# Last embedding phase in two column halves, and weight slabs laid out by the host

## The chip, the cores and the metric

The kernel runs on the 8 cores of one Trainium2 chip. Every core runs the same program on its own tokens, with the same weights read from the chip's memory. The metric is the device time of one execution in microseconds (us), which is that of the slowest core. Lower is better.

## The reference, cut to what matters

Each core holds 1044 token columns (1024 prompt tokens, 2 tokens of context, 16 sample tokens, 2 of padding). The two layers of the trunk are rows of these steps, D = 2048 wide:

```
h = h + 0.5 * swiglu(rmsnorm(h), ffn1)      # hidden width 5632
h = h + mixer(rmsnorm(h))                   # layer 0: chunked gMLP, layer 1: short convolution
h = h + 0.5 * swiglu(rmsnorm(h), ffn2)
gate = sigmoid(rmsnorm(h) @ ple_w_gate[i])  # 2048 x 2048
h = h + gate * (p[i] @ ple_w_proj[i])       # 256 x 2048
...
y = rmsnorm(h, final_norm)                  # after layer 1 alone
```

The last two statements of layer 1 and the final norm are what the change is about. A norm needs the sum of squares over all 2048 channels of a token, but no other token.

## The kernel before, in words

The state h lies on the chip, channels on partitions, as 16 channel blocks of 128 x 1044 float32. All projections are matmuls with a 128x128 block of weights as the stationary operand and token columns as the moving one. Every instruction is issued in the order of the program on its engine, and semaphore waits come from a record of the memory that each instruction reads and writes (class `Sync`).

**Feed-forward phases** (`ffn`) use a seven-product scheme on 2x2 blocks, with 261 columns per matmul; their weights are already laid out by the host so that each partition's part of a load is contiguous.

**All other projections** ("std" entries of `plan`) read a slab per output block: 2048 x 128 weights of one output block (or 256 x 128 for `ple_w_proj`), float32 in memory, converted to bf16 by the load. The source of one slab is a strided cut of a row-major matrix, so the longest contiguous piece is 128 floats, 512 bytes. Three slots hold slabs. `wget` (L385) for entry i first issues the loads up to entry i + 2 (`wpump`), and all these loads are issued from the POOL queue (L371). The slot of entry i + 2 is that of entry i - 1, so that load waits on the queue for the matmuls of entry i - 1. Whatever else POOL has to do stands in the same queue.

**The embedding phase** (`ple`, L797) runs over 16 output blocks d. In each: the gate group of 16 x 3 matmuls of 348 columns into banks 0 to 2; three products on DVE with the norm's scale into `sig`; a sigmoid on ACT; the projection group of 2 x 3 matmuls into banks 3 to 5; three products on DVE into `pletmp`; one addition on DVE into h; a square on ACT (L454); one addition on DVE into `acc` (L455). In block 0 the norm of the phase (`norm_all`) is placed between matmuls 12 and 13 of the gate's 16 k-steps, over all 1044 columns.

**The end** (L1128 to L1139): after block 15 the final norm over 1044 columns (`norm_all`), then per channel block one 1044-wide product with gain and scale, 11 of them on DVE and 5 on POOL after a scaling on ACT, and a store of 128 x 1044 float32 for each from the SP queue.

Of the kernel before, what the change touches and what calls it, by code (L numbers as in the profile page):

```python
# [6 lines left out]
F32 = mybir.dt.float32  # L7
BF16 = mybir.dt.bfloat16
F16 = mybir.dt.float16
AF = mybir.ActivationFunctionType  # L10
ALU = mybir.AluOpType

D = 2048
DFF = 5632
NCH = 16
NF = 44
DPLE = 256
# [6 lines left out]
TH = 1044  # L24
NH = TH // 2
NS = NH // 2
# [6 lines left out]
EPS = 1e-6  # L33
# [7 lines left out]
G_FIN = 13  # L41
# [115 lines left out]
def build_program():  # L157
    nc = bass.Bass("TRN2", target_bir_lowering=False, dynamic_dma_scratch_size=SCRATCH)

    def din(name, shape):  # L160
        return nc.dram_tensor(name, list(shape), F32, kind="ExternalInput").ap()
# [12 lines left out]
    for nm in ("ffn1", "ffn2"):  # L174
        for l in range(2):
            wd[nm, "g", l] = din("%s_g%d" % (nm, l), (NF // 2, 128, 4096))
            wd[nm, "u", l] = din("%s_u%d" % (nm, l), (NF // 2, 128, 4096))
            wd[nm, "d", l] = din("%s_d%d" % (nm, l), (DFF * D,))
    wd["a_in"] = din("a_w_in", (1, D, 2 * D))
    wd["a_out"] = din("a_w_out", (1, D, D))  # L180
    wd["c_in"] = din("c_w_in", (1, D, 3 * D))
    wd["c_out"] = din("c_w_out", (1, D, D))
    wd["ple_g"] = din("ple_w_gate", (2, D, D))
    wd["ple_p"] = din("ple_w_proj", (2, DPLE, D))
    wst_in = din("wst_in", (128, 8 * 128))
    a_b_s = din("a_b_s", (1, 8, 128))

# [15 lines left out]
    def view(name, shape, dt, off):  # L203
        names[name] = names.get(name, 0) + 1
        return nc.alloc_sbuf_tensor_at("%s_v%d" % (name, names[name]), [128] + list(shape), dt, offset=off)
# [65 lines left out]
    def plan_ple(l):  # L271
        for d in range(NCH):
            plan_std("ple_g", l, 0, 16, d * 128)
            plan_std("ple_p", l, 0, 2, d * 128)
# [16 lines left out]
        plan_std("c_out", 0, 0, 16, d * 128)  # L291
    plan_ffn("ffn2", 1)
    plan_ple(1)

    with contextlib.ExitStack() as es:
        S = Sync(nc, es)
# [25 lines left out]
        def act(out, a, func, more=(), **kw):  # L322
            S.op("act", [a, *more], [out], lambda: nc.scalar.activation(out=out, in_=a, func=func, **kw))  # L323
# [4 lines left out]
        def store(key, dst, a):  # L328
            S.dma("sp", [a], [], key, lambda: nc.sync.dma_start(out=dst, in_=a))
# [12 lines left out]
        def wissue(early=None):  # L342
            i = wst["issued"] if early is None else early
            ent = plan[i]
            if i in place_of:
                wst["issued"] += 1
                return
            if ent[0] == "std":
                _, name, l, k0, nk, c0 = ent
                if plan[i - 1][0] == "ffn":  # L350
                    wst["nstd"] = 0
                s = wst["nstd"] % 3
                wst["nstd"] += 1
                t = view("wsl", [16, 128], BF16, SLOT[s])
                src = wd[name][l].rearrange("(k p) c -> p k c", p=128)[:, k0:k0 + nk, c0:c0 + 128]
                dst, key = t[:, 0:nk, :], ("wl", s)
            else:
                _, nm, kind, l, nk, j = ent
                if i == 0 or plan[i - 1][0] == "std":
                    wst["nffn"] = 0  # L360
                n = wst["nffn"]
                wst["nffn"] += 1
                s = (2, 0, 1)[n % 3]
                t = view("raw", [4, nk, 128], F16, RAW[s])
                if kind == "d":
                    f0, d = j
                    src = bass.AP(wd[nm, "d", l].tensor, f0 * 128 * D + d * nk * 512 * 128, [[nk * 512, 128], [1, nk * 512]])
                else:
                    src = wd[nm, kind, l][j]
                dst, key = t[:].rearrange("p a k c -> p (a k c)"), ("wr", s)  # L370
            S.dma("pool", [], [dst], key, lambda: nc.gpsimd.dma_start(out=dst, in_=src))  # L371
            for a, b in span_of(dst):
                owner[a:b] = i
            place_of[i] = t
            if early is None:
                wst["issued"] += 1
# [420 lines left out]
        def ple(l, xn, pT, mode):  # L797
            sig = [view("sig", [TH], F32, NEW[0] + i * VB) for i in range(2)]
            tmp = view("pletmp", [TH], F32, NEW[0] + 2 * VB)
            for d in range(NCH):  # L800
                ws = wget("std", "ple_g", l, 0, 16, d * 128)
                mm_group(ws, 16, xn, PA, tile_major=d > 0, mid=norm_all if d == 0 else None)
                if d > 0 and mode == "pe":
                    norm_mm(d - 1)
                sb = sig[d % 2]
                evac3(lambda ti, t0, tn: tt("dve", sb[:, t0:t0 + tn], bank(PA[ti], tn), rstdF[:, t0:t0 + tn], ALU.mult))
                act(sb[:], sb[:], AF.Sigmoid)
                ws = wget("std", "ple_p", l, 0, 2, d * 128)
                mm_group(ws, 2, pT, PB)
                nst["acc"] = acc_ple  # L810
                evac3(lambda ti, t0, tn: tt("dve", tmp[:, t0:t0 + tn], bank(PB[ti], tn), sb[:, t0:t0 + tn], ALU.mult))
                tt("dve", h[:, d, :], tmp[:], h[:, d, :], ALU.add)
                if d == NCH - 1 and l == 0:
                    ffn_begin()
                h_next(d)
                if mode == "pe":
                    norm_sq(d)
                else:
                    acc_sq(d)
            nst["pend"] = ("ffn", mode)  # L820

        def gmlp_setup(step, wmT, bias2, wsn, bsb, ident_f, tri_f):
            if step == 0:
                load(("g", 0), wsn[:].rearrange("p h t -> p (h t)"), wst_in)
                load(("g", 1), bsb[:].rearrange("p h t -> p (h t)"), bass.AP(a_b_s.tensor, 0, [[0, 128], [1, 8 * 128]]))
                load(("cst", 1), ident_f[:], identd)
                load(("cst", 2), tri_f[:], trid)
            elif step == 2:
                S.op("dve", [ident_f[:]], [ident_b[:]], lambda: nc.vector.tensor_copy(out=ident_b[:], in_=ident_f[:]))
                for hh in range(8):  # L830
                    tt("dve", wmT[:, hh, :], wsn[:, hh, :], tri_f[:], ALU.mult)
            elif step == 3:
                def emit():
                    last = None
                    for hh in range(8):
                        last = nc.tensor.matmul(ps[:, (S0, S1)[hh // 4], (hh % 4) * 128:(hh % 4 + 1) * 128], lhsT=ones_b[:],
                                                rhs=wmT[:, hh, :], start=True, stop=True)
                    return last
                S.op("pe", [wmT[:], ones_b[:]], [bank(S0), bank(S1)], emit)
                for c in range(NCH):  # L840
                    hh = c // 2
                    stt("dve", bias2[:, c, :], ps[:, (S0, S1)[hh // 4], (hh % 4) * 128:(hh % 4 + 1) * 128], gcol(G_LNB, c),
                        bsb[:, hh, :], ALU.mult, ALU.add, more=[gcol(G_LNB, c)])
# [279 lines left out]
        ffn("ffn2", 1, XA, HA)  # L1123
        pT = load_p(1, off + XNB)
        nst["spec"] = ("fin", G_FIN, None)
        ple(1, xn, pT, "acc")
        assert wst["used"] == len(plan)
        nst["pend"] = ("fin", "acc")  # L1128
        norm_all()

        yo = [view("yo", [TH], F32, AR + i * VB) for i in range(16)]
        for c in range(2, NCH, 3):
            act(yo[c][:], h[:, c, :], AF.Copy, more=[gcol(G_FIN, c)], scale=gcol(G_FIN, c))
        for c in range(NCH):
            if c % 3 == 2:
                tt("pool", yo[c][:], yo[c][:], rstdF[:], ALU.mult)
            else:
                stt("dve", yo[c][:], h[:, c, :], gcol(G_FIN, c), rstdF[:], ALU.mult, ALU.mult, more=[gcol(G_FIN, c)])
            store(("o", "y", c), y_out[c], yo[c][:])  # L1139
        S.finish()  # L1140
    return nc

# [10 lines left out]
def pair_blocks(w):  # L1153

    k, m = w.shape
    a = w.reshape(k // 256, 2, 128, m // 256, 2, 128)
    return np.ascontiguousarray(a.transpose(3, 2, 4, 1, 0, 5)).reshape(m // 256, 128, -1)


def down_blocks(w):  # L1160
# [86 lines left out]
```

How the kernel before makes its waits and increments, by code:

```python
    def _wait_all(self, eng, deps):  # L109
        kn = self.known[eng]
        for k, v in deps.items():
            if k == "pe" and eng == "pe":
                continue
            if kn.get(k, 0) >= v:
                continue
            self.engs[eng].wait_ge(self.sems[k], v)
            self._learn(eng, k, v)
# [15 lines left out]
    def op(self, eng, reads, writes, emit):  # L133
        rs, ws = self._spans(reads), self._spans(writes)
        self._waits(eng, rs, ws)
        inst = emit()
        self.cnt[eng] += 1
        inst.then_inc(self.sems[eng], 1)
        self._record(eng, self.cnt[eng], eng, rs, ws)
# [1 line left out]
    def dma(self, queue, reads, writes, semkey, emit):  # L141
        rs, ws = self._spans(reads), self._spans(writes)
        self._sem(semkey, "s_" + "_".join(str(k) for k in semkey))
        self._waits(queue, rs, ws)
        inst = emit()
        self.cnt[semkey] += 16
        inst.then_inc(self.sems[semkey], 16)
        self._record(semkey, self.cnt[semkey], queue, rs, ws)
        self.dma_events[semkey] = self.cnt[semkey]
```

## Time and profile before

| what | value |
|---|---|
| median of 3 runs | 4791.91 us (4788.62 to 5107.49) |
| profiled execution | 4784.54 us, span 4783.5 us on its slowest core |
| spans of the 8 cores | 4773.8 to 4783.5 us |
| mean granted TensorE clock | 0.98 of full |
| PE busy | 4552.1 us, 95% of the span |
| DVE, ACT, POOL busy | 64%, 26%, 12% |
| chain that ended last | PE 88%, DVE 5%, DMA 2%, ACT 2% |
| last embedding phase | 4585.2 to 4726.9 us (first gate matmul to the end of the last gate group) |
| the end after it | 4726.9 to 4783.5 us |

The busy shares say that TensorE (PE) is at work nearly all the time; DVE has slack on average, which says nothing of a single phase. The table's last two rows are places in the timeline of the slowest core; the rows further down show them.

### The profile page before, as it was taken

To read this page: it belongs to the slowest core of one execution; us is meant where nothing else is said; L and a number is where in the kernel's file an instruction comes from. 1 tells how busy PE (TensorE), PEld (TensorE's weight loads), DVE (VectorE), ACT (ScalarE), POOL (GpSimd) and SP (SyncE) were. 2 spreads that over 40 slices of the span, in tenths; PEclk is the share of its full clock that TensorE was granted. 3 is DMA by queue.
4 is the path that set the end of the run, shared out by engine and by line. 5 is a ranking of instruction groups with operands and counts; after the bars stand their busy time and mean duration, and the time that the engine had idled before them with its cause. 6 is when DMAs were issued, how large, how long until landed. Compare 5 with 4: busy or idle time off the path is not lost.

```text
span 4783.5 us, 93347 instructions; the slowest of 8 cores (4773.8 to 4783.5 us)
## 1 busy us (share of the span) xinstructions
PE 4552.1 (95%) x37150; PEld 3623.5 (76%) x37150; DVE 3063.8 (64%) x5317; ACT 1234.1 (26%) x1857; POOL 571.5 (12%) x707
## 2 busy tenths in 40 slices
PE   6999999997999999999999999999999999999985
PEld 4888888764668888886588888886666788888863
DVE  6666666635566666666766666665445666666666
ACT  3222222525122222225222222232001222222342
POOL 0100110110101101101101110111111011101022
PEclk8999999998999999999999999999999999999997
DMA  5444545573754445444735444446778454454356
GB/s 126 80 73 87 89 73 93 71 71 33 67 76 85 72 84 89 81 88 61 77 70 96 77 82 80 87 78 68 75 71 83 74 89 80 73 93 84 73 66 107
DMA packets 360810, 380.57 MB, mean 80 GB/s; under 512 B 311984, under 2 KB 312624, under 8 KB 337840
## 3 DMA queue, kind: packets, MB, share of 16 engines
q0 software_dynamic: 355744, 359.80, 50.4%
q1 hardware_dynamic: 4640, 14.81, 1.1%
q8 instruction: 303, 4.96, 0.4%
q14 instruction: 123, 1.01, 0.1%
HBM read 721.22 MB, written 8.96 MB: 153 GB/s over the span
## 4 chain that ended last, share of the span: by engine, by line
PE 88%; DVE 5%; DMA 2%; ACT 2%; issue 2%; DVEq 0%; POOL 0%; ACTq 0%; SPq 0%; POOLq 0%
PE ps L567 67%; PE ps L403 19%; DMA wsl_v<-ple_w_gate 1%; DVE buf_v L315 1%; DVE st_v L910 1%; DVE yo_v L315 1%; ACT vhb_v L919 0%; ACT tb_v L323 0%; DVE tb_v L311 0%; DMA raw_v<-ffn_g 0%; ACT L323 0%; DVE hop_v L311 0%; DVE nw_v L311 0%; DVE h_v L311 0%; DMA h_v<-xin 0%
## 5 line engine op out<-in xcount | busy, mean ns | idle before, releaser
L567 PE MATMUL ps<-xop_v,raw_v 128*128 128x261 f16 x11264 | 1382.1, 276 | 16.3 <-DVE xop_v L315 7.5
L567 PEld LDWEIGHTS ps<-xop_v,raw_v 128*128 128x128 f16 x11264 | 1102.9, 98 | 207.1 <-issue 25.6
L567 PE MATMUL ps<-xop_v,nw_v 128*128 128x261 f16 x8448 | 1059.6, 277 | 20.9 <-ACT ps L323 14.5
L567 PEld LDWEIGHTS ps<-xop_v,nw_v 128*128 128x128 f16 x8448 | 828.1, 98 | 163.9 <-issue 25.4
L403 PE MATMUL ps<-xn_v,wsl_v 128*128 128x348 bf16 x5376 | 825.0, 315 | 35.7 <-DVE sig_v L311 15.5
L403 PEld LDWEIGHTS ps<-xn_v,wsl_v 128*128 128x128 bf16 x5376 | 526.1, 98 | 328.0 <-issue 43.4
L567 PE MATMUL ps<-hop_v,raw_v 128*128 128x261 f16 x5632 | 725.0, 276 | 18.5 <-DVE h_v L311 9.9
L323 ACT ACTIVATE tb_v<-ps 128x522 f32<-128x522 f32 x696 | 417.8, 604 | 873.1 <-PE ps L567 872.5
L311 DVE TENSOR_TENSOR h_v<-ps,h_v 128x522 f32<-128x522 f32 (+1 forms) x736 | 494.4, 675 | 229.0 <-PE ps L567 136.4
L567 PEld LDWEIGHTS ps<-hop_v,raw_v 128*128 128x128 f16 x5632 | 545.5, 98 | 120.9 <-issue 30.0
L567 PE MATMUL ps<-hop_v,nw_v 128*128 128x261 f16 x4224 | 558.4, 276 | 10.0 <-ACT tb_v L323 7.8
L567 PEld LDWEIGHTS ps<-hop_v,nw_v 128*128 128x128 f16 x4224 | 409.9, 98 | 86.9 <-issue 19.6
L323 ACT ACTIVATE ps<-ps 128x522 f32<-128x522 f32 x312 | 183.8, 589 | 889.8 <-PE ps L567 825.4
L323 ACT ACTIVATE tb_v<-tb_v 128x522 f32<-128x522 f32 x352 | 224.2, 639 | 689.0 <-DVE tb_v L311 689.0
L311 DVE TENSOR_TENSOR tb_v<-ps,rstdF_v 128x522 f32<-128x522 f32 x172 | 120.7, 702 | 349.2 <-PE ps L567 349.2
L311 DVE TENSOR_TENSOR tb_v<-ps,tb_v 128x522 f32<-128x522 f32 x356 | 248.8, 699 | 113.8 <-PE ps L567 111.8
L311 POOL TENSOR_TENSOR h_v<-tb_v,h_v 128x522 f32<-128x522 f32 x160 | 181.6, 1135 | 1139.2 <-ACT tb_v L323 1134.1
L315 DVE SCALAR_TENSOR_TENSOR sgr_v<-tb_v,rstdF_v 128x522 f16<-128x522 f32 x352 | 244.7, 696 | 29.1 <-ACT tb_v L323 28.7
L311 DVE TENSOR_TENSOR hop_v<-ps,sgr_v 128x522 f16<-128x522 f32 x176 | 123.4, 701 | 197.7 <-PE ps L567 197.7
L311 DVE TENSOR_TENSOR h_v<-tb_v,h_v 128x522 f32<-128x522 f32 x180 | 126.6, 703 | 185.5 <-ACT tb_v L323 185.5
L403 PE MATMUL ps<-buf_v,wsl_v 128*128 128x348 bf16 x1536 | 232.1, 313 | 10.6 <-DVE buf_v L311 6.2
L323 ACT ACTIVATE sqt_v<-h_v 128x1044 bf16<-128x1044 f32 (+1 forms) x141 | 150.5, 1067 | 321.9 <-DVE h_v L311 321.6
(126 smaller groups left out, 2946.8 us busy)
## 6 DMA issues: line engine op xcount, KB each, us to landing
raw_v<-ffn_g POOLq DMA_DIRECT2D x88, 1024.0 KB, 8.9
raw_v<-ffn_u POOLq DMA_DIRECT2D x88, 1024.0 KB, 8.8
raw_v<-ffn_d POOLq DMA_DIRECT2D x96, 512.0 KB, 5.6
raw_v<-ffn_d POOLq DMA_DIRECT2D x64, 640.0 KB, 6.4
wsl_v<-c_w_in POOLq DMA_DIRECT2D x48, 512.0 KB, 7.0
wsl_v<-a_w_in POOLq DMA_DIRECT2D x32, 512.0 KB, 6.9
wsl_v<-ple_w_gate POOLq DMA_DIRECT2D x32, 512.0 KB, 6.9
y<-yo_v SPq DMA_DIRECT2D x16, 522.0 KB, 7.1
```

What stands on the lines that cost most here:

```text
L311: S.op(eng, [a, b], [out], lambda: e.tensor_tensor(out=out, in0=a, in1=b, op=op))
L315: S.op(eng, [a, b, *more], [out], lambda: e.scalar_tensor_tensor(out=out, in0=a, scalar=scalar, in1=b, op0=op0, op1=op1))
L323: S.op("act", [a, *more], [out], lambda: nc.scalar.activation(out=out, in_=a, func=func, **kw))
L403: last = nc.tensor.matmul(ps[:, pset[ti], 0:tn], lhsT=ws[:, k, :], rhs=rhs[:, k, t0:t0 + tn], start=(k == 0), stop=(k == nk - 1))
L567: last = nc.tensor.matmul(ps[:, 2 * s + a, 0:NS], lhsT=lhs[:, k, :], rhs=rhs[:, k, a * NS:(a + 1) * NS], start=(start and k == 0), stop=(k ...
L910: S.op("dve", [bank((S0, S1)[q // 2])], [st6[jj][:, q, :]], lambda q=q: nc.vector.bn_stats(out=st6[jj][0:n, q, :], in_=pv[q // 2][0:n, (q ...
```

## The change

The last embedding phase is replaced by `ple_last`. It walks over the 16 blocks twice, each time for one half of the token columns (522 of 1044). Each half-step has a gate group of 16 x 2 matmuls of 261 columns, alternating between banks 0, 1 and banks 2, 3, and a projection group of 2 x 2 matmuls in banks 4 and 5; the DVE and ACT work is of half width. Each slab is loaded twice, once in each pass (`plan_ple(1)` stands twice in the plan).

The final norm of the first half is placed inside the first gate group of the second pass. The outputs of the first half are made in half-steps 2 to 15 of the second pass: even channel blocks on DVE, odd ones with a scaling on ACT and a product on POOL, each followed by its store. For four blocks of the second half the scaling on ACT is made early. After the second pass only the second half's norm, 16 half-width products (12 on DVE, 4 on POOL) and 16 half-width stores are left.

For `a_w_in`, `a_w_out`, `c_w_in`, `c_w_out`, `ple_w_gate` and `ple_w_proj` the host now writes each slab as 128 contiguous rows, so that a partition's part is one piece of 8192 bytes (1024 bytes for `ple_w_proj`).

```diff
-    wd["a_in"] = din("a_w_in", (1, D, 2 * D))
+    wd["a_in"] = din("a_w_in", (1, 2 * NCH, 128, D))
...
     plan_ple(1)
+    plan_ple(1)
...
-                src = wd[name][l].rearrange("(k p) c -> p k c", p=128)[:, k0:k0 + nk, c0:c0 + 128]
-                dst, key = t[:, 0:nk, :], ("wl", s)
+                src = wd[name][l][c0 // 128]
+                dst, key = t[:, 0:nk, :].rearrange("p k c -> p (k c)"), ("wl", s)
...
+        def ple_last(xn, pT):
...
+            def last_norm(p):
...
+                for b, c0 in ((S0, a), (S1, a + NS)):
+                    S.op("pe", [acc_ple[:, c0:c0 + NS], mean_f[:]], [bank(b, NS)], lambda b=b, c0=c0: nc.tensor.matmul(
+                        bank(b, NS), lhsT=mean_f[:], rhs=acc_ple[:, c0:c0 + NS], start=True, stop=True))
+                for b, c0 in ((S0, a), (S1, a + NS)):
+                    tsc("dve", sF[:, c0:c0 + NS], bank(b, NS), EPS, ALU.add)
+                act(rstdF[:, sl], sF[:, sl], AF.Ln)
+                act(rstdF[:, sl], rstdF[:, sl], AF.Exp, scale=-0.5)
+                act(t[:, sl], rstdF[:, sl], AF.Square, scale=0.5 ** 0.5)
+                act(rstdF[:, sl], rstdF[:, sl], AF.Copy, scale=-1.0)
+                tt("dve", sF[:, sl], sF[:, sl], t[:, sl], ALU.mult)
+                stt("dve", rstdF[:, sl], sF[:, sl], -1.5, rstdF[:, sl], ALU.add, ALU.mult)
+
+            def scaled(p, c):
+                act(yo[p][c][:], h[:, c, p * NH:(p + 1) * NH], AF.Copy, more=[gcol(G_FIN, c)], scale=gcol(G_FIN, c))
+
+            def output(p, c, eng):
+                sl = slice(p * NH, (p + 1) * NH)
+                if eng == "pool":
+                    tt("pool", yo[p][c][:], yo[p][c][:], rstdF[:, sl], ALU.mult)
+                else:
+                    stt("dve", yo[p][c][:], h[:, c, sl], gcol(G_FIN, c), rstdF[:, sl], ALU.mult, ALU.mult,
+                        more=[gcol(G_FIN, c)])
+                store(("o", "y", p, c), y_out[c][:, sl], yo[p][c][:])
+
+            every = [list(range(15)), [15]]
+            for p in range(2):
+                a = p * NH
+                sl = slice(a, a + NH)
+                for d in range(NCH):
+                    ws = wget("std", "ple_g", l, 0, 16, d * 128)
+                    banks = (0, 1) if d % 2 == 0 else (2, 3)
+                    if d == 0:
+                        group(ws, 16, xn, banks, a, [list(range(12))])
+                        norm_all() if p == 0 else last_norm(0)
+                        group(ws, 16, xn, banks, a, [[k] for k in range(12, 16)])
+                    else:
+                        group(ws, 16, xn, banks, a, every)
+                    sb = sig[d % 2]
+                    for b, c0 in zip(banks, (a, a + NS)):
+                        tt("dve", sb[:, c0:c0 + NS], bank(b, NS), rstdF[:, c0:c0 + NS], ALU.mult)
+                    act(sb[:, sl], sb[:, sl], AF.Sigmoid)
+                    ws = wget("std", "ple_p", l, 0, 2, d * 128)
+                    group(ws, 2, pT, (4, 5), a, [[0, 1]])
+                    for b, c0 in ((4, a), (5, a + NS)):
+                        tt("dve", tmp[:, c0:c0 + NS], bank(b, NS), sb[:, c0:c0 + NS], ALU.mult)
+                    tt("dve", h[:, d, sl], tmp[:, sl], h[:, d, sl], ALU.add)
+                    if d == 0:
+                        act(acc_ple[:, sl], h[:, d, sl], AF.Square)
+                    else:
+                        sq = sqs_std[d % 2]
+                        act(sq[:, 0:NH], h[:, d, sl], AF.Square)
+                        tt("dve", acc_ple[:, sl], sq[:, 0:NH], acc_ple[:, sl], ALU.add)
+                    if p == 1:
+                        for c in ([d - 2] if 2 <= d < 14 else [2 * d - 16, 2 * d - 15] if d >= 14 else []):
+                            if c % 2:
+                                scaled(0, c)
+                            output(0, c, "pool" if c % 2 else "dve")
+                    if p == 1 and d >= 6 and d % 3 == 0:
+                        scaled(1, d - 4)
+            last_norm(1)
+            for c in range(NCH):
+                output(1, c, "pool" if c in (2, 5, 8, 11) else "dve")
...
-        ple(1, xn, pT, "acc")
+        ple_last(xn, pT)
         assert wst["used"] == len(plan)
-        nst["pend"] = ("fin", "acc")
-        norm_all()
-
-        yo = [view("yo", [TH], F32, AR + i * VB) for i in range(16)]
-        for c in range(2, NCH, 3):
-            act(yo[c][:], h[:, c, :], AF.Copy, more=[gcol(G_FIN, c)], scale=gcol(G_FIN, c))
-        for c in range(NCH):
...
+def slabs(w):
+
+    l, k, m = w.shape
+    return np.ascontiguousarray(w.reshape(l, k // 128, 128, m // 128, 128).transpose(0, 3, 2, 1, 4)).reshape(l, m // 128, 128, k)
...
+        "a_w_in": slabs(f(a_w_in)), "a_w_out": slabs(f(a_w_out)), "c_w_in": slabs(f(c_w_in)), "c_w_out": slabs(f(c_w_out)),
+        "ple_w_gate": slabs(f(ple_w_gate)), "ple_w_proj": slabs(f(ple_w_proj)),
```

## Rows read from the trace of the kernel before

**Rows 1.** The page: chain that ended last, share of the span by engine.
```profile
PE 88%; DVE 5%; DMA 2%; ACT 2%; issue 2%; DVEq 0%; POOL 0%; ACTq 0%; SPq 0%; POOLq 0%
```
**Rows 2.** Windows (stretch, busy us and count by engine, clock, DMA share, GB/s).
```profile
3360.00:3420.00 60.00, 60.00 (x407) 39.09 (x405) 27.80 (x48) 0.00 (x0) 9.82 (x9) 1.00 0.74 71
4440.00:4500.00 60.00, 60.00 (x529) 51.55 (x527) 39.55 (x65) 13.86 (x23) 3.17 (x6) 1.00 0.45 82
1100.00:1140.00 40.00, 26.94 (x198) 19.21 (x199) 22.58 (x69) 20.12 (x31) 2.91 (x3) 0.79 0.42 40
```
**Rows 3.** Timeline, a step of the last phase (start, us, engine, work, idle before).
```profile
4644.97 1.57 DVE L311 TENSOR_TENSOR sig_v<-ps,rstdF_v 128x348 f32<-128x348 f32 x3
4646.13 7.24 PE L403 MATMUL ps<-xn_v,wsl_v 128*128 128x348 bf16 x48
...
4647.81 1.57 DVE L311 TENSOR_TENSOR pletmp_v<-ps,sig_v 128x348 f32<-128x348 f32 x3 [1.27 <-ACT sig_v L323]
...
4653.16 1.56 DVE L311 TENSOR_TENSOR sig_v<-ps,rstdF_v 128x348 f32<-128x348 f32 x3
4653.21 1.05 PE L403 MATMUL ps<-pT_v,wsl_v 128*128 128x348 bf16 x6
4653.79 0.70 POOL L371 DMA_DIRECT2D wsl_v<-ple_w_proj  x1 [5.61 <-PE ps L403]
4654.97 1.17 POOL L371 DMA_DIRECT2D wsl_v<-ple_w_gate  x1 [0.48 <-issue]
```
**Rows 4.** Chain that ended last, in order of time: one piece of the last phase.
```profile
4654.97 7.58 DMA wsl_v<-ple_w_gate
```
**Rows 5.** DMA issues: count, KB written, median us to landing; second: last phase alone.
```profile
raw_v<-ffn_d POOLq DMA_DIRECT2D x96, 512.0 KB, 5.6
wsl_v<-ple_w_gate POOLq DMA_DIRECT2D x16, 512.0 KB, 7.1
```
**Rows 6.** Groups by form, whole span (count, busy us, mean ns, idle before).
```profile
L311 DVE TENSOR_TENSOR h_v<-ps,h_v 128x522 f32<-128x522 f32 x640 | 447.4, 699 | 154.4 <-PE ps L567 136.4 <-DVE h_v L311 0.6 <-issue 0.2
L323 ACT ACTIVATE tb_v<-tb_v 128x522 f32<-128x522 f32 x352 | 224.2, 639 | 689.0 <-DVE tb_v L311 689.0
L311 POOL TENSOR_TENSOR h_v<-tb_v,h_v 128x522 f32<-128x522 f32 x160 | 181.6, 1135 | 1139.2 <-ACT tb_v L323 1134.1 <-PE ps L567 5.0
```
**Rows 7.** Timeline, start of the last phase.
```profile
4585.21 6.79 PE L403 MATMUL ps<-xn_v,wsl_v 128*128 128x348 bf16 x36 [4.64 <-DMA wsl_v<-ple_w_gate]
...
4602.81 1.56 DVE L311 TENSOR_TENSOR sig_v<-ps,rstdF_v 128x348 f32<-128x348 f32 x3
4603.58 9.58 PE L403 MATMUL ps<-xn_v,wsl_v 128*128 128x348 bf16 x48 [7.05 <-DVE sig_v L311]
...
4604.45 1.28 ACT L323 ACT_TABLE_LOAD   x1 [0.39 <-DVE sig_v L311]
```
**Rows 8.** Timeline, the end (first three); the tile yo: ns min/median/max.
```profile
4726.89 1.06 PE L403 MATMUL ps<-pT_v,wsl_v 128*128 128x348 bf16 x6
4735.31 4.00 PE L496 MATMUL ps<-acc_v,mean_f_v 128*128 128x512 f32 x6 [7.36 <-DVE acc_v L311]
4751.13 21.00 SPq L329 DMA_DIRECT2D y<-yo_v  x16
L315 DVE SCALAR_TENSOR_TENSOR yo_v<-h_v,colt_v,rstdF_v x11: 1293/1296/3526, 4747.5 to 4770.4; 128x1044 f32<-128x1044 f32 x11
```
**Rows 9.** PE's waits for slabs, whole span; second: last phase (us, times, longest).
```profile
PE ps L403 <- DMA wsl_v<-ple_w_gate: 9.8, 7, 4.6
...
PE ps L403 <- DMA wsl_v<-ple_w_gate: 5.9, 4, 4.6
...
PE ps L403 <- DMA wsl_v<-a_w_out: 4.2, 2, 3.2
PE ps L403 <- DMA wsl_v<-a_w_in: 2.9, 1, 2.9
...
PE ps L403 <- DMA wsl_v<-c_w_in: 1.5, 1, 1.5
```

More of the change, by code:

```diff
@@ L178, in build_program @@
             wd[nm, "d", l] = din("%s_d%d" % (nm, l), (DFF * D,))
-    wd["a_in"] = din("a_w_in", (1, D, 2 * D))
[L180 to L184, printed above, removed]
+    wd["a_in"] = din("a_w_in", (1, 2 * NCH, 128, D))
+    wd["a_out"] = din("a_w_out", (1, NCH, 128, D))
+    wd["c_in"] = din("c_w_in", (1, 3 * NCH, 128, D))
+    wd["c_out"] = din("c_w_out", (1, NCH, 128, D))
+    wd["ple_g"] = din("ple_w_gate", (2, NCH, 128, D))
+    wd["ple_p"] = din("ple_w_proj", (2, NCH, 128, DPLE))
     wst_in = din("wst_in", (128, 8 * 128))
@@ L820, in ple, with group, emit @@
             nst["pend"] = ("ffn", mode)
+        def ple_last(xn, pT):
+            l = 1
+            sig = [view("sig", [TH], F32, NEW[0] + i * VB) for i in range(2)]
+            tmp = view("pletmp", [TH], F32, NEW[0] + 2 * VB)
+            yo = [[view("yo", [NH], F32, AR + i * HV) for i in range(NCH)]] * 2
+            t = s2
+            def group(ws, nk, rhs, banks, a, ks):
+                for ti, b in enumerate(banks):
+                    c0 = a + ti * NS
+                    for sub in ks:
+                        def emit(sub=sub):
+                            last = None
+                            for k in sub:
+                                last = nc.tensor.matmul(bank(b, NS), lhsT=ws[:, k, :], rhs=rhs[:, k, c0:c0 + NS],
+                                                        start=(k == 0), stop=(k == nk - 1))
+                            return last
+                        S.op("pe", [ws[:, sub[0]:sub[-1] + 1, :]] + [rhs[:, k, c0:c0 + NS] for k in sub], [bank(b, NS)], emit)
+            def last_norm(p):
[24 more added lines that the diff above has]
+            for p in range(2):
+                a = p * NH
+                sl = slice(a, a + NH)
+                for d in range(NCH):
[32 more added lines that the diff above has]
+                output(1, c, "pool" if c in (2, 5, 8, 11) else "dve")
@@ L1125, in build_program @@
         nst["spec"] = ("fin", G_FIN, None)
-        ple(1, xn, pT, "acc")
+        ple_last(xn, pT)
         assert wst["used"] == len(plan)
-        nst["pend"] = ("fin", "acc")
-        norm_all()
-        yo = [view("yo", [TH], F32, AR + i * VB) for i in range(16)]
-        for c in range(2, NCH, 3):
-            act(yo[c][:], h[:, c, :], AF.Copy, more=[gcol(G_FIN, c)], scale=gcol(G_FIN, c))
-        for c in range(NCH):
[L1135 to L1139, printed above, removed]
         S.finish()
@@ L1193 @@
         "cols": cols, "ident": ident, "tri": tri,
-        "a_w_in": f(a_w_in), "a_w_out": f(a_w_out), "c_w_in": f(c_w_in), "c_w_out": f(c_w_out),
-        "ple_w_gate": f(ple_w_gate), "ple_w_proj": f(ple_w_proj),
+        "a_w_in": slabs(f(a_w_in)), "a_w_out": slabs(f(a_w_out)), "c_w_in": slabs(f(c_w_in)), "c_w_out": slabs(f(c_w_out)),
+        "ple_w_gate": slabs(f(ple_w_gate)), "ple_w_proj": slabs(f(ple_w_proj)),
         "a_b_s": f(a_b_s),
```

## The prediction

> **What bounds the kernel now.** I read the chain of waits first: TensorE holds 88% of it [rows 1], so only what shortens PE's work or its waits can pay. The busy windows give PE's pace: 407 matmuls of 348 columns in 60 us and 529 of 261 columns in 60 us [rows 2], 0.147 us and 0.113 us each, so a column costs nearly the same in either cut. Then the timeline of one step of the last embedding phase [rows 3]. Three loops run there, and all are about 8.2 us long. PE: 54 matmuls, 54 x 0.147 = 8.0 us. DVE, which does its work strictly in order and waits for ACT twice per step: from one `sig` to the next, 4644.97 to 4653.16, 8.19 us. Slabs: the gate slab of block d+2 is asked for after gate group d, lands, and its group runs; from the end of gate group d to the POOL instruction 1.76 us, 7.58 us to the landing [rows 4], 0.14 us, 7.1 us of group: 16.6 us for two steps, 8.3 us per step. So now everything just fits. The reader should see that halving the columns halves PE's and DVE's loop, but not the slab's: each pass reads all slabs again.
>
> From the first gate matmul at 4585.2 [rows 7] to the end of the last gate group at 4726.9 [rows 8] the phase takes 141.7 us, and the end after it to 4783.5 takes 56.6 us.
>
> **A half-step, priced.** PE: 36 x 0.1134 = 4.08 us, of which the gate group 3.63. DVE: a 261-wide product, on the line through 0.52 us at 348 [rows 3] and 0.70 at 522 [rows 6], costs 0.43; ACT at 522 takes 0.64, DVE 0.70 [rows 6]. The loop is 0.86 + 0.64 + 0.86 + 0.70 + 0.64 + 0.70 with six hand-overs of 0.08 to 0.1: 4.9 us. Slab: the host's layout makes a gate slab the same transfer as a 512 KB `ffn_d` load, which lands 5.6 us after its instruction starts, against 7.1 now [rows 5]; I take 5.6, with 5.1 (less traffic) and 7.1 (layout brings nothing) as ends. Ahead of it, from the end of a gate group, 0.58 to the projection slab's issue and about 1.0 for that issue (1.18 now [rows 3]): 1.6. Loop: 1.6 + 5.6 + 0.14 + 3.63 = 11.0 for two half-steps, **5.5 us each**. The slab loop, not PE (4.1) or DVE (4.9), sets the first pass.
>
> **The second pass has a new wait.** In half-steps 3, 5, ... 13 the product of an odd channel block stands in POOL's queue ahead of the next gate slab's issue. It waits for a scaling that stands on ACT behind the square, which waits for DVE's addition. From the end of the gate group: second `sig` 0.5, sigmoid 0.74, products 0.96, addition 0.8, square 0.74, scaling 0.75, POOL product 0.1 + 1.14 [rows 6]: 5.8 us instead of 1.6. Two half-steps then take 5.8 + 5.6 + 0.14 + 3.63 = 15.2 us; the even one in between fits inside. The stores on SP queue behind nothing else, and DVE's own 0.7 us output per second half-step is covered by this wait; ACT has room. If the wait were gone, DVE's output would cost 0.7 on every second half-step.
>
> **The phase.** The first pass: norm matmuls after 24 x 0.113 = 2.7 us instead of 6.6 (36 matmuls in 6.79, the last one's tail overlapped [rows 7]), so DVE's first `sig` comes at 17.6 - 3.9 = 13.7 us [rows 7]; first `sig` 0.9, table load 1.28 [rows 7], sigmoid 0.8, products 0.9, projection group 0.5 and gate group 3.6 end at 21.6; 13 more at 5.5: 93. The second pass: block 0 with two half-width norm matmuls (4.0 us for full width [rows 8], so 1.75) 7.3; the norm holds DVE about 5 us, some 2 of it past the slack; three half-steps of 5.5; six pairs of 15.2: 117. Sum 210 against 141.7: **+68**.
>
> **The clock.** The third of [rows 7] shows the price of a long pause: after 7.05 us without matmuls the next 48 took 9.58 us, not 7.24, as the granted clock was partly at half (1.2 of 2.4 GHz). Where a stage has pauses of 2 to 3 us at about 70% busy, the mean clock was 0.79 [rows 2]. The second pass has six pauses of about 7 us (15.2 less 8.2 of work): 6 x 2.3 = 14; the first pass, pauses of up to 3 us per pair, between 0 and 1.6 a pair, taken as 5 in all. **+19**, ends 5 and 70 (below). The Trainium skill, "TensorE: Matmul & The Clock Gate", section "HAM oscillation", says that a kernel whose matmuls per tile are shorter than the wait for the tile's data is throttled again at every tile; by that rule the clock's share would be that of the third rival.
>
> **The end.** From the last gate group to the norm's first matmul 8.4 us now, half-width 4.6 (0.5 + 0.74 + 0.96 + 0.8 + 0.74 + 0.8); the norm 12.2 (4735.3 to 4747.5 [rows 8]), half 7.4 (4.0 of matmuls become 1.75, six 1044-wide passes lose 0.45 each, the table load stays); then from the first product to the end 36.0. There the stores are the limit: 8.55 MB in the 32.4 us from the first store [rows 8], 264 GB/s; half is 16.2, plus 0.8 for the first product and 2 for landing: 19. Twelve DVE products of 0.65 to 0.75 and four on POOL, 14 us even if they exclude each other, hide behind it (DVE's products took 1.3 alone and up to 3.5 beside POOL's [rows 8]). 31 against 56.6: **-25**. The first half's 16 stores lie inside the second pass, beside slab loads: at 264 GB/s 1 us of every 7.6, covered.
>
> **Host layout elsewhere.** PE's waits for slabs outside this phase are 9.8 - 5.9 (this phase's own share) + 4.2 + 2.9 + 1.5 = 12.5 us [rows 9], all that faster slabs can give; some are first slabs of a phase that only land 1.5 us sooner. I take **-8**, and -1.5 for the last phase's own first slab (4.64 us of wait [rows 7]). Shorter POOL issue (1.17 to about 0.55) sits under PE in those stages. Ends 0 and -13.
>
> **Sum** against the profiled execution of 4784.5: 68 + 19 - 25 - 8 - 1.5 = +52, 4837. The runs' median is 7 above that execution and their lowest 4; with 6 of it: **4843 us**, +1.1%.
>
> **Rivals.**
>
> 1. *Not slower: the slabs don't set the pace, DVE does.* It decides if a gate slab can be used within 2 x 4.9 - 3.63 = 6.2 us of the earlier gate group's end, in the second pass too, where POOL would have to be free in time. Then 85 + 88 = 173 us, +32, and without clock loss and with the full 12.5 elsewhere: 32 - 25 - 13 - 1.5 = -7, 4784. For it: contiguous slabs, and only 5.9 us of slab waits now. Against: 1.6 + 5.1 is already 6.7, and the POOL product alone comes at 5.8. Chance 0.10. The Trainium skill, "DMA: Bandwidth & Descriptors", section "Anatomy of one DMA", has 2.0 us plus bytes over 436 GB/s for such a load, 4.4 us for this one, an estimate by which the first pass would meet this condition; the same-sized row took 5.6, and the measurement decides.
> 2. *The slab loop paces, but POOL's product is early enough.* Second pass 7.3 + 2 + 15 x 5.5 = 92: 185 in all, +43, clock 5: +14, 4804. For it: POOL's additions in the feed-forward phases wait 1134 us for ACT [rows 6] with loads queued behind them, and PE hardly notices; against: there a load is not needed as soon as it can be asked for, here it is. Chance 0.12.
> 3. *The clock stays at half through the phase.* Gate groups of 7.26 us, 8.2 us per half-step on PE; first pass 21.6 + 4 + 13 x 8.2 = 132, second pass 8.2 + 3.5 + 3 x 8.2 + 6 x (5.8 + 5.74 + 7.26) = 149: +139 - 25 - 9.5 = +105, 4895. Against: at 8.2 us per half-step PE would be busy all the time, and busy stages ran at 1.00 [rows 2]. Chance 0.10.
> 4. *The layout doesn't do what it should:* slabs land after 7.1 us as now. Loops 6.2 and 16.7: 102 + 128 = 230, +89; clock 20, end -25, nothing elsewhere: +84, 4874. Against: `ffn_d`. Chance 0.10.
>
> **Numbers.** My forecast has 0.55, its own range 4818 to 4872 (landing 5.1 to 6.2, clock 5 to 35, layout 0 to -13); 0.03 is for something unseen, mostly small. The range from 4798 to 4884 takes in the forecast, rival 2 and rival 4. The 2% bound (96 us, 4888 and 4696), about what a measurement of this kernel can tell from no change, is passed upwards by rival 3 and a little of rival 4: 0.12. Faster by 2%: 0.01. Within: 0.87.
>
> **What would show it.** In the timeline of the second pass, gate groups 5, 7, ... 15 preceded by PE waits of about 7 us for `ple_w_gate`, POOL's `yo` product right before each issue, and pairs 15 us apart; in the first pass 11 us per pair; slabs landing in 5.6; granted clock between 0.7 and 0.9; first to last gate group 210 to 235 us; 31 us after it; no slab waits in the other phases. I am wrong if PE waits in the phase mostly name DVE, if slabs land in under 5 us, or if the other phases change by more than 13 us.

## The result, and the profile after

The changed kernel is slower than the kernel before by 1.3%: ratio 1.013, 95% interval 1.008 to 1.018. The profiled execution took 4848.17 us against 4784.54, 64 us more; forecast were 4843 us and 52 us more against the profiled execution. The change of 1.3% is inside the 2% to which the prediction gave 0.87. In most executions of the runs below the cores of one half of the chip (0 to 3 or 4 to 7) or of both had a lower granted clock throughout, so a time without another name is the median of the slowest core of a half that had not, over three to seven such executions.

The first thing to read is again which engine holds the chain that ended last. First busy time, then the chain, from the page of the changed kernel; they answer to the table of before and to [rows 1].

```profile
PE 4567.1 (94%) x37423; PEld 3660.8 (76%) x37440; DVE 3067.2 (63%) x5392; ACT 1245.7 (26%) x1902; POOL 493.9 (10%) x746
...
PE 86%; DVE 5%; DMA 4%; ACT 3%; issue 2%; DVEq 0%; POOL 0%; ACTq 0%; SPq 0%; POOLq 0%
```

PE's busy time grew by 15 us of the 64; the rest is time in which PE stood, and DMA's share of the chain doubled. The waits say for what. These are PE's waits in the last phase and after it (us in all, times, longest), which answer to [rows 9]:

```profile
PE ps L838 <- DMA wsl_v<-ple_w_gate: 71.0, 18, 9.3
PE ps L838 <- DVE pletmp_v L312: 12.6, 2, 7.9
PE ps L847 <- DVE acc_v L312: 6.2, 2, 4.4
```

71 us of waiting for gate slabs where there were 5.9. The timeline of PE in the first pass shows the norm's first matmuls, then gate groups (32 matmuls) and projection groups (4), with the wait ahead of each in brackets:

```profile
4575.85 3.78 PE L497 MATMUL ps<-acc_v,mean_f_v 128*128 128x512 f32 x6 [1.87 <-DVE acc_v L312]
...
4600.47 3.75 PE L838 MATMUL ps<-xn_v,wsl_v 128*128 128x261 bf16 x32 [1.38 <-DMA wsl_v<-ple_w_gate]
4604.05 0.61 PE L838 MATMUL ps<-pT_v,wsl_v 128*128 128x261 bf16 x4
4606.03 3.75 PE L838 MATMUL ps<-xn_v,wsl_v 128*128 128x261 bf16 x32 [1.37 <-DMA wsl_v<-ple_w_gate]
4609.62 0.61 PE L838 MATMUL ps<-pT_v,wsl_v 128*128 128x261 bf16 x4
4611.00 3.75 PE L838 MATMUL ps<-xn_v,wsl_v 128*128 128x261 bf16 x32 [0.77 <-DMA wsl_v<-ple_w_gate]
```

From 4600.47 to 4611.00 two half-steps take 10.5 us; the last thirteen of the pass took 6.0 us each on this core and 5.3 to 5.7 on the others. In the second pass the timeline of all engines shows the new wait; this is the stretch from one late gate group to the next (columns as before):

```profile
4717.42 6.38 PE L838 MATMUL ps<-xn_v,wsl_v 128*128 128x261 bf16 x32 [5.57 <-DMA wsl_v<-ple_w_gate]
4723.64 0.61 PE L838 MATMUL ps<-pT_v,wsl_v 128*128 128x261 bf16 x4
...
4727.10 0.64 ACT L324 ACTIVATE sqt_v<-h_v 128x522 bf16<-128x522 f32 x1 [1.97 <-DVE h_v L312]
4727.65 0.72 ACT L324 ACTIVATE yo_v<-h_v,colt_v 128x522 f32<-128x522 f32 x1
4727.67 0.61 PE L838 MATMUL ps<-pT_v,wsl_v 128*128 128x261 bf16 x4
...
4728.51 1.28 POOL L312 TENSOR_TENSOR yo_v<-yo_v,rstdF_v 128x522 f32<-128x522 f32 x1 [3.75 <-ACT yo_v L324]
...
4729.74 0.59 POOL L372 DMA_DIRECT2D wsl_v<-ple_w_gate  x1
...
4730.85 0.55 POOL L372 DMA_DIRECT2D wsl_v<-ple_w_gate  x1
...
4736.54 5.38 PE L838 MATMUL ps<-xn_v,wsl_v 128*128 128x261 bf16 x32 [8.25 <-DMA wsl_v<-ple_w_gate]
```

The reader should follow it backwards. The group at 4736.54 waited for a slab whose load was issued at 4729.74, and that load stood in POOL's queue behind the product of 4728.51, which stood waiting for ACT's scaling of 4727.65, behind the square, behind DVE. The earlier group ended at 4723.6, so 6.1 us passed to the issue and 6.8 more to the use. The late groups start at 4717.42, 4736.54, 4754.73, 4774.60, 4793.53 and 4812.27: pairs of 18.2 to 19.9 us. The late group itself takes 5.38 us instead of 3.75, after 8.25 us without matmuls. The windows of the two passes and the end (PE busy, clock, DMA share, GB/s) show the granted clock, which was 0.79 in the stage with pauses in [rows 2]:

```profile
4571.00:4677.00 106.00, 76.98 (x585) 0.90 0.57 93
4677.00:4822.00 145.00, 82.25 (x583) 0.81 0.46 88
4822.00:4847.00 25.00, 2.08 (x4) 0.50 0.52 193
```

The loads of the last phase, with the median us to landing over both passes, answer to [rows 5]:

```profile
wsl_v<-ple_w_gate POOLq DMA_DIRECT2D x32, 512.0 KB, 6.3
y<-yo_v SPq DMA_DIRECT2D x32, 261.0 KB, 2.9
wsl_v<-ple_w_proj POOLq DMA_DIRECT2D x32, 64.0 KB, 3.5
```

The end, as in [rows 8]: the norm's first matmul, the last products on POOL and DVE, and DVE's products of the whole run (ns min/median/max).

```profile
4822.23 2.08 PE L847 MATMUL ps<-acc_v,mean_f_v 128*128 128x261 f32 x4 [4.44 <-DVE acc_v L312]
...
4830.21 5.69 POOL L312 TENSOR_TENSOR yo_v<-yo_v,rstdF_v 128x522 f32<-128x522 f32 x4 [6.30 <-DVE rstdF_v L316]
4830.24 11.60 DVE L316 SCALAR_TENSOR_TENSOR yo_v<-h_v,colt_v,rstdF_v 128x522 f32<-128x522 f32 x12 [0.17 <-DVE rstdF_v L316]
...
L316 DVE SCALAR_TENSOR_TENSOR yo_v<-h_v,colt_v,rstdF_v x20: 750/756/1640, 4703.4 to 4841.1; 128x522 f32<-128x522 f32 x20
```

Single cores start the phase 14 us (before) and 16 us (after) apart, so parts of the kernel are best compared as means over the eight cores of the two profiled executions: start of the last phase 4578.2 before and 4567.8 after (-10.4 us); from its first gate matmul to the final norm's first matmul 150.5 and 244.2 (+93.7); from there to the end 49.9 and 26.4 (-23.5). Together +60; the slowest cores differ by 64.

### The profile page after: what moved, and what is told of

The parts are those of the page before. It is cut to its first block, busy times and chain, and to the rows that moved or that the text cites. A ratio compares the mean times of both kernels' runs of the same rounds, so it can differ in the third digit from the quotient of the medians.

```text
span 4847.1 us, 94370 instructions; the slowest of 8 cores (4831.4 to 4847.1 us)
## 1 busy us (share of the span) xinstructions
PE 4567.1 (94%) x37423; PEld 3660.8 (76%) x37440; DVE 3067.2 (63%) x5392; ACT 1245.7 (26%) x1902; POOL 493.9 (10%) x746
## 4 chain that ended last, share of the span: by engine, by line
PE 86%; DVE 5%; DMA 4%; ACT 3%; issue 2%; DVEq 0%; POOL 0%; ACTq 0%; SPq 0%; POOLq 0%
PE ps L568 66%; PE ps L404 17%; DMA wsl_v<-ple_w_gate 2%; PE ps L838 2%; DMA raw_v<-ffn_g 1%; DVE buf_v L316 1%; DVE st_v L997 1%; ACT tb_v L324 0%; ACT vhb_v L1006 0%; ACT L324 0%; DVE h_v L312 0%; DVE tb_v L312 0%; DMA h_v<-xin 0%; DVE hop_v L312 0%; DVE nw_v L312 0%
## 5 line engine op out<-in xcount | busy, mean ns | idle before, releaser
L404 PE MATMUL ps<-xn_v,wsl_v 128*128 128x348 bf16 x4608 | 701.7, 314 | 18.4 <-DVE sig_v L312 8.4
L404 PEld LDWEIGHTS ps<-xn_v,wsl_v 128*128 128x128 bf16 x4608 | 450.0, 98 | 264.9 <-issue 22.2
L316 DVE SCALAR_TENSOR_TENSOR sgr_v<-tb_v,rstdF_v 128x522 f16<-128x522 f32 x352 | 244.2, 695 | 29.2 <-ACT tb_v L324 28.8
L324 ACT ACTIVATE sqt_v<-h_v 128x1044 bf16<-128x1044 f32 (+2 forms) x156 | 153.5, 984 | 327.3 <-DVE h_v L312 327.2
```

The source lines that it names most:

```text
L404: last = nc.tensor.matmul(ps[:, pset[ti], 0:tn], lhsT=ws[:, k, :], rhs=rhs[:, k, t0:t0 + tn], start=(k == 0), stop=(k == nk - 1))
```

## The experiments

**What is to be told apart.** My theory: in two passes the way of a slab from its issue to its use sets the pace, and in the second pass POOL's product stands ahead of that issue. Rivals: DVE's in-order chain (4.9 us per half-step) or the clock is the pace and slab waits only follow it; the transfers' rate is the limit; POOL's work itself costs, wherever it stands, for instance by slowing DVE's instructions beside it (1.3 us alone and up to 3.5 beside POOL's in [rows 8]). Two parts of the change are first taken alone. The kernel before took 4791.3 us (4786.2 to 4796.0) beside the first four runs, 4789.1 (4785.9 to 4796.2) beside the next four.

**The layout alone.** The kernel before with the host's slabs (the load's part of the edit):

```diff
-                src = wd[name][l].rearrange("(k p) c -> p k c", p=128)[:, k0:k0 + nk, c0:c0 + 128]
-                dst, key = t[:, 0:nk, :], ("wl", s)
+                src = wd[name][l][c0 // 128]
+                dst, key = t[:, 0:nk, :].rearrange("p k c -> p (k c)"), ("wl", s)
```

> The kernel before with the host's contiguous slabs and nothing else. My theory (slabs cost PE only the few waits that name them, 12.5 us outside the last phase and 5.9 in it): 8 to 16 us under the kernel before, about 4780; slab landing in the last phase 5.6 to 6.3 us instead of 7.1, PE's waits for slabs in all phases together under 6 us. Rival A (the layout speeds everything by relieving memory): more than 25 us under, under 4765. Rival B (the layout brings nothing, the change in the other phases was another thing): within 3 us of the kernel before.

Measured: 4772.1 us (4769.0 to 4773.6), 19 under the kernel before; the range expected was 8 to 16. PE's waits for slabs on cores 4 to 7 fell from 11 to 19 us to 3 to 5 us. First the loads in the last phase on core 5, then PE's only slab wait of the whole span there:

```profile
wsl_v<-ple_w_gate POOLq DMA_DIRECT2D x15, 512.0 KB, 5.4
wsl_v<-ple_w_proj POOLq DMA_DIRECT2D x16, 64.0 KB, 2.3
...
PE ps L403 <- DMA wsl_v<-ple_w_gate: 2.7, 1, 2.7
```

What follows: the layout is a gain. The slab waits that it removes are 6 to 16 us on these cores; the rest of the 19 is not accounted for. Most of it lies ahead of the last phase, which starts at 4568.5 on the mean of cores 4 to 7 (4567.9 in the changed kernel, 4579.7 before) and takes 148.5 to 149.2 us to the norm's first matmul, against 150.1 to 150.9. So the changed kernel's gain in the other phases is the layout's. Slabs landed after 5.1 to 6.3 us in the median of each of these cores, against 6.5 to 7.1.

**The halves alone.** The changed kernel with the old strided slabs (the reverse of the diff above).

> The changed kernel with the old strided slabs: two passes, no host layout. My theory (the slab's way from issue to use sets both passes): slabs land in 7.5 to 9 us, half-steps of 6.5 to 7 in the first pass, pairs of 19 to 21 in the second, the phase 25 to 40 us longer than in the changed kernel, and 10 more in the other phases: 4880 to 4905. Rival (DVE's chain and the clock set the pace, slab waits are only what they show up as): the phase within 8 us of the changed kernel, time 4855 to 4865.

Measured: 4881.0 us (4875.2 to 4883.5), 90 over the kernel before and 35 over the changed one. The phase took 258 to 268 us on cores 4 to 7, against 241 to 245. Two half-steps of the first pass (PE's timeline):

```profile
4623.48 5.41 PE L838 MATMUL ps<-xn_v,wsl_v 128*128 128x261 bf16 x32 [2.57 <-DMA wsl_v<-ple_w_gate]
4628.73 0.61 PE L838 MATMUL ps<-pT_v,wsl_v 128*128 128x261 bf16 x4
4630.22 3.75 PE L838 MATMUL ps<-xn_v,wsl_v 128*128 128x261 bf16 x32 [0.88 <-DMA wsl_v<-ple_w_gate]
4633.80 0.61 PE L838 MATMUL ps<-pT_v,wsl_v 128*128 128x261 bf16 x4
4637.05 5.42 PE L838 MATMUL ps<-xn_v,wsl_v 128*128 128x261 bf16 x32 [2.63 <-DMA wsl_v<-ple_w_gate]
```

13.6 us per pair, 6.8 per half-step, where the changed kernel has 5.3 to 6.0. So a slower slab slows the first pass, as the theory wants and a pace set by DVE excludes. The second pass did not get slower, which the theory did not want. From the phase's start to the second pass's norm the run took 119 to 124 us (99 to 106 in the two profiled executions of the changed kernel, cores 4 to 7), from there to the final norm's first matmul 139 to 145 (140 to 144). Two late groups of the second pass:

```profile
4765.71 5.99 PE L838 MATMUL ps<-xn_v,wsl_v 128*128 128x261 bf16 x32 [7.14 <-DMA wsl_v<-ple_w_gate]
...
4786.37 5.91 PE L838 MATMUL ps<-xn_v,wsl_v 128*128 128x261 bf16 x32 [9.22 <-DMA wsl_v<-ple_w_gate]
```

A late slab was used 7.3 us after its issue on the mean, against 7.1 to 7.3 with the contiguous slabs: at that place the layout brought nothing. Why, no run shows. The phase lost 20 us, less than the 25 I gave as the low end: slabs landed after 6.6 us, not 7.5 or more.

**All first-half products on DVE.**

```diff
-                            if c % 2:
-                                scaled(0, c)
-                            output(0, c, "pool" if c % 2 else "dve")
+                            output(0, c, "dve")
```

> The changed kernel with all 16 first-half products on DVE, none on POOL, and no scaling on ACT for them; same results. My theory (POOL's product holds the next gate slab back by 4.2 us in half-steps 3 to 13, which costs 12 half-steps some 2.5 to 3.5 us each): pairs in the second pass fall from 18.7 to 11.5 to 13 us, the time by 30 to 40 us: 4808 to 4820. Rival (DVE sets the second pass, and takes on 0.75 us more in every second half-step): no gain, or 5 us slower: 4848 to 4855.

Measured: 4807.0 us (4799.9 to 4811.0). The changed kernel, run again beside the second group, took 4846.1 (4841.3 to 4852.2): 39 less. PE's waits for gate slabs fell from 65 to 72 us to 34 to 37 on cores 4 to 7, and this is a pair of the second pass, 4711.84 to 4723.40, 11.6 us instead of some 19:

```profile
4711.84 5.17 PE L838 MATMUL ps<-xn_v,wsl_v 128*128 128x261 bf16 x32 [3.38 <-DMA wsl_v<-ple_w_gate]
4716.85 0.61 PE L838 MATMUL ps<-pT_v,wsl_v 128*128 128x261 bf16 x4
4717.30 3.75 PE L838 MATMUL ps<-xn_v,wsl_v 128*128 128x261 bf16 x32
4720.88 0.61 PE L838 MATMUL ps<-pT_v,wsl_v 128*128 128x261 bf16 x4
4723.40 3.75 PE L838 MATMUL ps<-xn_v,wsl_v 128*128 128x261 bf16 x32 [1.91 <-DMA wsl_v<-ple_w_gate]
```

DVE got more work and the kernel got 39 us faster, so DVE's work did not set the second pass.

**The changed kernel again**, as a reference.

> The changed kernel unaltered, as the reference for the three beside it. Both theories: 4840 to 4850, the phase from its first gate matmul to the final norm's first matmul 240 to 250 us.

Measured: 4846.1 us; phase 242 to 246 us on cores 4 to 7.

**The product behind the issue.** POOL keeps its products; each is only moved behind the next gate slab's issue (in part):

```diff
                     ws = wget("std", "ple_g", l, 0, 16, d * 128)
+                    while queued:
+                        output(0, queued.pop(0), "pool")
...
                                 scaled(0, c)
-                            output(0, c, "pool" if c % 2 else "dve")
+                                queued.append(c)
+                            else:
+                                output(0, c, "dve")
```

> The changed kernel with three slots and POOL's products kept, but each product stands behind the issue of the next gate slab in the program instead of ahead of it; same results. My theory (what costs is only the place in POOL's queue, not POOL's work): as with the products on DVE, pairs in the second pass of 12 to 13.5 us instead of 18.7, time 4803 to 4815. The product now stands ahead of the next projection slab's issue, which is asked for 4 us later, so it may give 2 to 5 us of that back. Rival (POOL's work itself, through the port it shares with DVE, is what costs): above 4830.

Measured: 4809.1 us (4805.5 to 4816.7), as with no POOL product at all. So it is the place in the queue that costs 37 us. Against the run with the products on DVE there are 2 us, 4 if each is counted from the kernel before beside it; their spreads overlap. The rival that POOL's work itself costs, put at above 4830, is out.

**Eight slots instead of three.** Five more slots lie in memory that is free in the last phase, and loads are issued seven entries ahead instead of two (in part):

```diff
+    LAST = len(plan)
     plan_ple(1)
     plan_ple(1)
...
-                s = wst["nstd"] % 3
+                s = wst["nstd"] % (8 if i >= LAST else 3)
...
-            wpump(i + 2)
+            wpump(i + (7 if i >= LAST else 2))
```

> The changed kernel with eight slab slots in the last phase instead of three (five more in memory that is free then) and loads issued seven entries ahead instead of two; same results, POOL's products stay. My theory (what counts is the time from issue to use, not the rate of the transfers): PE's waits for slabs in the last phase go from 71 us to under 10, half-steps become DVE's 4.9 to 5.5, the phase falls from 244 to 180 to 190: 4785 to 4798. Rival (the transfers' rate is the limit, all eight cores reading 1.1 MB per half-step): half-steps stay above 5.5 and the time above 4815.

Measured: 4792.7 us (4788.4 to 4794.1), phase 188 to 190 us. The same bytes now move in 55 us less, so the rate of the transfers was not the limit. Loads landed no sooner (6.0 to 6.9 us in the median of cores 4 to 7, 5.9 to 6.4 in the changed kernel), and PE hardly waited for them. PE's waits in the phase now name DVE:

```profile
PE ps L840 <- DVE pletmp_v L314: 27.5, 23, 7.9
...
PE ps L840 <- DMA wsl_v<-ple_w_gate: 1.0, 1, 1.0
```

And DVE's chain is full, with a wait for ACT before the second and the fourth of its steps (second pass, timeline):

```profile
4706.26 0.95 DVE L314 TENSOR_TENSOR sig_v<-ps,rstdF_v 128x261 f32<-128x261 f32 x2
...
4708.05 0.96 DVE L314 TENSOR_TENSOR pletmp_v<-ps,sig_v 128x261 f32<-128x261 f32 x2 [0.83 <-ACT sig_v L326]
...
4709.11 0.70 DVE L314 TENSOR_TENSOR h_v<-pletmp_v,h_v 128x522 f32<-128x522 f32 x1
...
4710.65 0.70 DVE L314 TENSOR_TENSOR acc_v<-sqt_v,acc_v 128x522 f32<-128x522 bf16 x1 [0.83 <-ACT sqt_v L326]
4711.27 0.95 DVE L314 TENSOR_TENSOR sig_v<-ps,rstdF_v 128x261 f32<-128x261 f32 x2
```

4706.26 to 4711.27 is 5.0 us: the 4.9 of the prediction.

**Eight slots and all first-half products on DVE** (both diffs above).

> Eight slots and all first-half products on DVE; same results. My theory (with eight slots DVE's chain of 4.9 us paces both passes, and POOL's products no longer stand in anything's way): every half-step of the second pass gains a DVE output of 0.7 instead of every other one, so this is 3 to 6 us slower than eight slots alone, 4793 to 4800. Rival (POOL's products still cost something behind the queue or at DVE's port): 5 to 10 us faster than eight slots alone.

Measured: 4794.6 us (4792.7 to 4797.2), 2 more than with eight slots alone; phases 192 to 195 us against 188 to 190. As expected, where slabs are not late, moving the products off POOL costs a little instead of gaining 39.

**Eight slots and another order on DVE.** The addition of block d-1's squares and the output come while ACT makes block d's sigmoid (in part):

```diff
                     act(sb[:, sl], sb[:, sl], AF.Sigmoid)
+                    while adds:
+                        adds.pop(0)()
+                    outs(p, d)
                     ws = wget("std", "ple_p", l, 0, 2, d * 128)
...
-                        tt("dve", acc_ple[:, sl], sq[:, 0:NH], acc_ple[:, sl], ALU.add)
+                        adds.append(lambda sq=sq, sl=sl: tt("dve", acc_ple[:, sl], sq[:, 0:NH], acc_ple[:, sl], ALU.add))
```

> Eight slots, first-half products on DVE, and DVE's order changed: the addition of the squares of block d-1 and the output come after the first products of block d, in the time in which ACT makes the sigmoid; same results. My theory (with the slabs out of the way DVE's in-order chain is the pace, 4.9 to 5.6 us of which 1.7 is waiting for ACT; filled, its work of 3.3 to 4.1 us fits under PE's 4.1): half-steps of 4.1 to 4.4 us, phase 155 to 165 us, 4752 to 4766, under both kernels and under the layout alone (4772). Rival (transfers at 1.1 MB per 4.1 us and core are then too slow, or the matmuls of 261 columns run below their pace): half-steps of 4.8 or more, 4775 or above.

Measured: 4762.8 us (4760.7 to 4769.7), phase 158 to 163 us. That is 26 under the kernel before and 83 under the changed kernel; the layout alone was 19 under the kernel before beside it, so this is 7 to 9 better still: the two passes pay once both waits are gone, if only by so much. DVE's timeline has no wait for ACT left:

```profile
4702.45 0.69 DVE L314 TENSOR_TENSOR acc_v<-sqt_v,acc_v 128x522 f32<-128x522 bf16 x1
...
4703.06 0.76 DVE L318 SCALAR_TENSOR_TENSOR yo_v<-h_v,colt_v,rstdF_v 128x522 f32<-128x522 f32 x1
4703.73 0.96 DVE L314 TENSOR_TENSOR pletmp_v<-ps,sig_v 128x261 f32<-128x261 f32 x2
4704.79 0.70 DVE L314 TENSOR_TENSOR h_v<-pletmp_v,h_v 128x522 f32<-128x522 f32 x1
4705.41 0.42 DVE L314 TENSOR_TENSOR sig_v<-ps,rstdF_v 128x261 f32<-128x261 f32 x1
...
4706.49 0.69 DVE L314 TENSOR_TENSOR acc_v<-sqt_v,acc_v 128x522 f32<-128x522 bf16 x1
```

4702.45 to 4706.49 is 4.04 us, with DVE nearly without a gap.

**The new order with three slots.** The control of the last one: products on DVE and the new order, but the changed kernel's slots.

> Two passes with the new DVE order and all first-half products on DVE, but with the three slots of the changed kernel; same results. My theory (with three slots the slab's way from issue to use, 11 us per two half-steps, is above DVE's chain, so emptying the chain gives nothing): phase 195 to 206 us as with the products on DVE alone, 4798 to 4808. Rival (DVE's chain is the pace and the slab waits only follow it): 4765 to 4780.

Measured: no time that can be compared. The phase itself ran near the usual clock (0.93 and 0.89 in its two passes on core 6, as in the run with the products on DVE: 0.95 and 0.90) and can be compared: 205 to 214 us on all eight cores, against 200 to 212 with the products on DVE alone, and 158 to 166 with eight slots. The 195 to 206 expected were missed by up to 8 us. PE waits for slabs on core 6:

```profile
PE ps L838 <- DMA wsl_v<-ple_w_gate: 33.5, 19, 3.3
```

A shorter DVE chain gives nothing while slabs are late. By the phase, though without a time, this is the sharpest refutation of DVE as the pace.

**One pass, the layout and the new order**, to see whether the order alone would do:

> The kernel before, in one pass, with the host's layout and with DVE's addition of squares moved behind the next block's first products; same results. My theory (in one pass, with slabs on time, DVE's chain of 8.19 us per step is just above PE's 7.96, so filling it frees 0.2 us per step): the phase 2 to 4 us shorter than with the layout alone, 4767 to 4771. Rival (the order alone is what made the eight-slot two-pass kernel fast, passes or not): 4755 to 4762.

Measured: again no time that can be compared. The phase took 145.0 to 146.5 us on cores 4 to 7, against 148.5 to 149.2 with the layout alone: the 3 us expected. (On cores 0 to 3, with a lower mean clock of 0.94 in the phase, it took 148 to 149.) If they reach the end, that makes some 4769, above the eight-slot kernel; as a time this is inferred, not measured.

## Why the prediction was right

The direction, the size and the mechanism held. The phase came out 10 us longer than its sum, mostly by the landing of the late slabs, and part of the closeness is luck, as shown below. By its own steps:

- **First pass.** Forecast 93 us and 5 for the clock; measured 98 on the mean of the eight cores and 105 on the profiled one (4571.1 to 4676.6). The mean is right by two errors of opposite sign. The start, up to the end of the third gate group, was put at 21.6 and took 26.7 (27.5 on the profiled core): the norm's first matmul came 4.7 us into the phase, not 2.7, since it waited for DVE's last addition of squares, and its six matmuls took 3.78 us where the kernel before had 2.01; so DVE's first `sig` came after 17.3 us, not 13.7, and the gate group behind it was a slow one (5.36 us). The other thirteen half-steps took 71.5 us with all losses of clock, where 71.5 and the 5 for the clock were forecast. Between 4585 and 4668 their slabs landed after 5.5 to 5.8 us in the median of each core: the 5.6 of the `ffn_d` row was right.
- **Second pass.** The new wait was where it was put, and was removed by moving the product in the queue (4846 to 4809). In the stretch shown it is 6.1 us from gate group to issue, forecast 5.8, and 6.8 from issue to use. Over 40 such slabs on the eight cores the way from issue to use is 7.1 us on the mean (6.3 to 8.5), forecast 5.7. This is the term that was too small. The cause of the slower landing stays open. Two gate slabs and a projection slab are issued there within 1.2 us, but that alone is not it: with all products on DVE the gate slabs of the second pass are issued 4 us and more apart and still landed after 6.6 to 6.9 us in the median of cores 4 to 7, against 5.3 to 6.0 in that run's first pass. What is also new in the second pass are the stores of the first half; no run takes them away. Pairs of 18.2 to 19.9, forecast 15.2 + 2.3 = 17.5.
- **The clock.** Twelve gate groups took 4.9 to 6.5 us instead of 3.75, together 20.7 us more than at full clock; forecast 19. It was worked out from one row of 7.05 us pause, and the third rival, half clock throughout, did not come: the mean was 0.90 and 0.81. The Trainium skill ("TensorE: Matmul & The Clock Gate", section "HAM oscillation") ties the loss to a wait that is longer than the matmuls of a tile. In the second pass the trace agrees: each of the six waits of 5.6 to 9.3 us, longer than a gate group, was followed by a slow group. In the first pass no wait for a slab was longer than a gate group, and still three of the ten were followed by a slow one (those of 2.25, 2.86 and 3.22 us, while one of 3.74 was not), as was one after 2.81 us in the second.
- **The end.** Forecast -25 us from the last gate group on; measured 29.8 us against 56.6, -27. The amount was right but not the reason: the stores are no longer the limit. DMA was busy for half of that time; the chain that ended last runs through DVE's twelve products of 11.6 us, and the end comes 5 us after the last of them.
- **The other phases.** Forecast -8 and -1.5; measured -10.4 at the start of the last phase.
- **The sum.** Means over the eight cores: phase up to the norm's first matmul +83 forecast (68 + 19 - 3.8), +94 measured; from there on -21 and -23.5; elsewhere -9.5 and -10.4. Of the 10 us too few, the six late pairs make 9 (114.3 us, forecast 91 and 14 for the clock) and the start of the first pass 5, and its other half-steps give 5 back. On the profiled core the last gate group ended 246 us after the first one's start (236 to 246 over the cores), outside the 210 to 235 that the prediction had named as a sign, and its pairs are 18 to 20 us apart, not 15. That 4843 and 4848 are so close is partly luck: this core's phase was 17 us longer than forecast, and it started the phase 14 us earlier instead of 9.5 and gained 2 us more at the end; 6 of the 11 us that are left were covered by the 6 added to reach the runs' median.

The experiments made rivals 1, 2 and 4 come about. Rival 2 (POOL's product not in the way), put at 4804, is the run with the product behind the issue: 4809. Rival 4 (landing as slow as now), put at 4874, is near the run with the halves alone: 4881 (landing 6.6 us there). Rival 1 (only DVE sets the pace), 4784, is the run with eight slots: 4793. Its mechanism is there; the phase is some 10 us longer than it was put at, of which 4 lie in the start of the first pass (25.6 us on the mean of cores 4 to 7, put at 21.6). DVE's loops are 5.0 and 5.7 us for 4.9 and 5.6, and the mean clock was 0.96 and 0.92, for which nothing was charged.

## What to carry to other kernels

Cutting this phase in halves halved every loop in it except the one that loads its weights; before such a cut write each loop down (issue, landing, use; DVE's chain with its waits; PE's groups) and see which one does not shrink. In an engine's queue that also issues loads, ask of every instruction that waits for another engine what load stands behind it: here a product of 1.3 us per pair of half-steps, in the wrong place, cost 37 us in all. When a load is late, look for slots and lead before bandwidth: five more slots took away 53 us with the same bytes.

## What the runs showed that I had not expected

DVE's in-order chain was the hidden second limit, 32 us (4794.6 to 4762.8), invisible in the waits of the changed kernel and plain as soon as the slabs were on time. The strided slabs, which cost the first pass some 20 us, cost the second pass nothing. And the issue of a strided slab held POOL for 1.17 us against 0.53 for the contiguous one; in one pass PE waited for slabs in this phase for only 1.4 to 5.9 us in all on each core, so little of that difference can have reached it.
